# The sample tokens' mLSTM recurrence moved from a phase of its own into the head loop of the mLSTM phase, with y passed to the output projection through DRAM

## The reference, cut to what matters

```python
# prompt: 16 chunks of 64 tokens in the reference, state starts at zero
# sample: one chunk of 4 tokens for each of 8 sequences, state comes in as state_C, state_n, state_m
num = w_inter[..., None] * einsum('bhvk,bhjk->bhjv', c, qc) + einsum('bhjs,bhsv->bhjv', a, vc)
den = w_inter * einsum('bhk,bhjk->bhj', n, qc) + sum(a, axis=-1)
h = num / maximum(abs(den), exp(-mj))[..., None]
c_new = decay[..., None, None] * c + einsum('bhs,bhsv,bhsk->bhvk', wg, vc, kc)
n_new = decay[..., None] * n + einsum('bhs,bhsk->bhk', wg, kc)
# then, in the layer:
hc = head_rmsnorm(sigmoid(o) * h, hnorm)
x + (hc * silu(z)) @ w_out_a
```

## Time and profile before

| what | value |
|---|---|
| median of 3 runs | 1976.89 us (1974.68 to 1979.36) |
| the profiled execution | 1973.47 us, of which its span is 1971.8 us |
| TensorE busy over the span | 1775.7 us (90%) |
| VectorE / ScalarE / GpSimd busy | 1069.3 (54%) / 761.8 (39%) / 458.5 us (23%) |
| the head loop of the mLSTM phase | about 39 to 684 us |
| the sample phase | about 684 to 801 us |
| output projection, then the rest | 801 us to the end |

### The profile page before, as it was taken

How to read it: one execution, slowest core, us unless ns; L and a number is a source line. 1 busy time by engine, 2 the same in 40 slices (tenths; PEclk the granted TensorE clock), 3 DMA queues, 4 the chain that set the end, 5 groups by cost and what they waited for, 6 DMA issues and landing times. The chain is left out here.

```text
span 1971.8 us, 37984 instructions
## 1 busy us (share of the span) xinstructions
PE 1775.7 (90%) x12147; PEld 1584.6 (80%) x12147; DVE 1069.3 (54%) x2885; ACT 761.8 (39%) x2040; POOL 458.5 (23%) x863
## 2 busy tenths in 40 slices
PE   4899999999999768797999999999999688888698
PEld 4789999999899756576998999999999666666385
DVE  4653443543543444425666666666665466767543
ACT  5333333333333212313335344344353356666511
POOL 1121221221212212012324334244242100101101
PEclk8899999999999966798999999999999798989799
DMA  5203213213121033612111211211200267676532
GB/s 156 68 3 67 38 30 68 36 32 68 7 61 15 4 90 95 206 43 92 34 35 43 55 34 32 66 34 32 65 13 11 95 234 265 237 273 232 159 127 87
DMA packets 146957, 164.83 MB, mean 84 GB/s; under 512 B 12730, under 2 KB 118042, under 8 KB 146898
## 3 DMA queue, kind: packets, MB, share of 16 engines
q1 hardware_dynamic: 142594, 159.85, 27.0%
q0 software_dynamic: 1184, 4.23, 0.8%
q10 hardware_dynamic: 3120, 0.01, 0.1%
HBM read 138.69 MB, written 25.37 MB: 83 GB/s over the span
## 5 line engine op out<-in xcount | busy, mean ns | idle before, releaser
L820 PE MATMUL PS<-WH,XH 128*128 128x384 f32 (+3 forms) x1152 | 370.0, 321 | 0.0
L820 PE MATMUL PS<-WL,XH 128*128 128x384 f32 (+3 forms) x1152 | 357.3, 310 | 0.0
L820 PE MATMUL PS<-WH,XL 128*128 128x384 f32 (+3 forms) x1152 | 357.3, 310 | 0.0
L820 PEld LDWEIGHTS PS<-WH,XH 128*128 128x128 f32 (+1 forms) x1152 | 208.8, 181 | 4.5
L820 PEld LDWEIGHTS PS<-WL,XH 128*128 128x128 f32 (+1 forms) x1152 | 208.8, 181 | 4.1
L820 PEld LDWEIGHTS PS<-WH,XL 128*128 128x128 f32 (+1 forms) x1152 | 208.2, 181 | 4.6
L1890 PE MATMUL PD<-WH,XH 128*128 128x256 f32 (+1 forms) x576 | 169.9, 295 | 2.9 <-PEq L142 2.9
L1890 PE MATMUL PS<-WH,XH 128*128 128x256 f32 (+1 forms) x576 | 168.3, 292 | 0.2 <-ACT WORK L1625 0.2
L1890 PE MATMUL PD<-WL,XH 128*128 128x256 f32 (+1 forms) x576 | 164.2, 285 | 0.0
L1890 PE MATMUL PD<-WH,XL 128*128 128x256 f32 (+1 forms) x576 | 163.7, 284 | 0.0
L1890 PE MATMUL PS<-WL,XH 128*128 128x256 f32 (+1 forms) x576 | 162.3, 282 | 0.0
(11 more groups left out here) (361 smaller groups left out, 4152.7 us busy)
## 6 DMA issues: line engine op xcount, KB each, us to landing
RAW<-in_cache_k SPq DMA_DIRECT2D x64, 512.0 KB, 4.6
WORK<-in_cache_v SPq DMA_DIRECT2D x64, 512.0 KB, 4.5
RAW<-in_w_in_a SPq DMA_DIRECT2D x40, 512.0 KB, 6.2
RAW<-in_w_in_b SPq DMA_DIRECT2D x16, 512.0 KB, 6.3
RAW<-in_w_kv SPq DMA_DIRECT2D x16, 512.0 KB, 5.3
out<-RAW SPq DMA_DIRECT2D x12, 512.0 KB, 3.8
out<-WORK SPq DMA_DIRECT2D x12, 512.0 KB, 3.2
WORK<-in_x_prompt SPq DMA_DIRECT2D x8, 512.0 KB, 4.4
```

The lines of the kernel that those rows point to most:

```text
L820: last = nc.tensor.matmul(bank[0:rows, 0:n], x[:, k, tt], reg(w)[:, k, :], start=(i == 0), stop=(i == 3 * KT - 1))
```

## The change

`mlstm_sample_phase` is gone. Its work for head h is cut into pieces that each engine runs inside sweep1 of head h + 1, at fixed blocks t; head 7, which has no next head, runs its pieces one after the other behind the loop (`last_head`). `SS` stays in SBUF and is no longer stored. The states are loaded to `CI` and updated in place, so the next load waits for the store. Since the space of `YT` now holds the sample buffers, each head's y is collected in `YS` (1056 columns), stored to DRAM by GpSimd (`s_store`, `d_yA`), and read back by `out_phase` along with the weights. SP's loop is peeled for head 0. In the diff, pieces that only copy or scale small tiles (`s_gates`, `s_inter`, `s_square`, `s_queries`, `s_divide`, `s_gate`) are left out; they hold the instructions of the old phase with other buffers.

```diff
+                        if first:
+                            sp.wait_ge(g_col, 1)
+                            sp.dma_start(GS[0:TS, :, :], d_G[:, SEQ:TOK].partition_broadcast(TS)).then_inc(b_k, 16)
+                            sp.dma_start(HNS, hnorm_a[0, :].partition_broadcast(P)).then_inc(b_k, 16)
+                        else:
+                            sp.wait_ge(b_st, 16 * h)
+                        sp.dma_start(CI, state_C[0, :, bass.ds(h, 1), :, :].rearrange("b a v k -> v (b a) k")).then_inc(b_c, 16)
                         if not last:
                             sp.wait_ge(lo1, KT * (h + 1))
                             load1(h + 1)
-                        sp.wait_ge(ss, h + 1)
-                        sp.dma_start(d_smA[:, :, bass.ds(h * P, P)], SS[0:TS, :, :]).then_inc(a_sst, 16)
...
+                            if before is not None:
+                                if t == 0:
+                                    tail(before)
+                                    s_gates(before)
+                                if t == 2:
+                                    s_state(before)
+                                if t == 6:
+                                    s_inter(before)
+                                if t == 7:
+                                    s_square(before)
...
+                    def s_state(h):
+                        act.wait_ge(b_qt, h + 1)
+                        act.activation(QT2, BK[4][:, 0:2 * TS].rearrange("p (a t) -> p a t", a=2), ACT.Copy)\
+                           .then_inc(b_qe, 1)
+                        act.wait_ge(b_ctp, h + 1)
+                        act.activation(CT[:, 0:4, 0:P], BK[5].rearrange("p (b v) -> p b v", b=4), ACT.Copy)
+                        act.activation(CT[:, 4:8, 0:P], BK[7].rearrange("p (b v) -> p b v", b=4), ACT.Copy).then_inc(b_cte, 1)
...
+                            if t == 3:
+                                s_gate(before)
+                        s_root(before)
...
+                    def s_root(h):
+                        pool.wait_ge(b_sq, h + 1)
+                        apart(pool)
+                        slinks.link(g.tensor_scalar(svar[0:TS, :], sss[0:TS, :], 4.0 / P, 16 * EPS, ALU.mult, ALU.add))
+                        g.tensor_tensor(srs[0:TS, :], svar[0:TS, :], neg_half[0:TS, :], ALU.pow).then_inc(b_rr, 1)
+                        pool.wait_ge(b_cn, h + 1)
+                        pool.dma_start(c_s[0, :, bass.ds(h, 1), :, :].rearrange("b a v k -> v (b a) k"), CI).then_inc(b_st, 16)
+                    def s_store(h):
+                        pool.wait_ge(b_yte, h + 1)
+                        pool.dma_start(d_yA[bass.ds(h, 1), :, :].rearrange("a p t -> (a p) t"), YS).then_inc(a_yst, 16)
+                    def last_head(h):
+                        s_gate(h)
+                        s_root(h)
+                        s_store(h)
+                        pool.wait_ge(b_nev, 1)
+                        pool.dma_start(n_s[0, :, :, :].rearrange("b h k -> (b h) k"), nN[0:DB * H, :]).then_inc(b_nst, 16)
+                        pool.wait_ge(b_st, 16 * H)
+                        pool.wait_ge(a_yst, 16 * H)
+                        pool.wait_ge(b_nst, 16)
+                    def sweep2(h, last, first=False):
+                        if not first:
+                            s_store(h - 1)
...
-                        v.tensor_copy(YT[:, bass.ds(h, 1), c * P:(c + 1) * P].rearrange("p a c -> p (a c)"),
-                                      BK[2 + c % 2][:, 0:P]).then_inc(tr_free[c % 2], 1)
+                        v.tensor_copy(YS[:, c * P:(c + 1) * P], BK[2 + c % 2][:, 0:P]).then_inc(tr_free[c % 2], 1)
...
+                    def s_weight(h):
+                        hh = bass.ds(h, 1)
...
+                        v.tensor_tensor(VW[0:TS, :, :],
+                                        SS[0:TS, 2, :].unsqueeze(1).to_broadcast([TS, DB, P]),
+                                        WG[0:TS, :].unsqueeze(2).to_broadcast([TS, DB, P]), ALU.mult).then_inc(b_vw, 1)
...
+                    def s_update(h):
+                        hh = bass.ds(h, 1)
+                        dve.wait_ge(b_ex, h + 1)
+                        dve.wait_ge(b_s, h + 1)
...
+                        v.tensor_tensor(nO[:, :, hh].rearrange("p b a -> p (b a)"), nM, BK[4][:, 64:64 + DB], ALU.add)
+                        v.scalar_tensor_tensor(sAT[0:TS, :], BK[4][0:TS, 0:TS], K_SCALE, sEX[0:TS, :],
+                                               ALU.mult, ALU.mult).then_inc(b_at, 1)
+                        dve.wait_ge(b_upd, h + 1)
+                        for s in range(DB):
+                            bank = BK[5] if s < 4 else BK[7]
+                            last_one = v.scalar_tensor_tensor(CI[:, s, :], CI[:, s, :],
+                                                              DEC[:, bass.ds(h * 2 * NT + NT + s, 1)],
+                                                              bank.rearrange("p (b k) -> p b k", b=4)[:, s % 4, :],
+                                                              ALU.mult, ALU.add)
+                        last_one.then_inc(b_cn, 1)
...
+                    def s_output(h):
+                        dve.wait_ge(b_rr, h + 1)
+                        dve.wait_ge(b_gz, h + 1)
+                        v.scalar_tensor_tensor(sY[0:TS, :], sU[0:TS, :], srs[0:TS, :], sGZ[0:TS, :],
+                                               ALU.mult, ALU.mult).then_inc(b_y, 1)
+                    def s_transposed(h):
+                        dve.wait_ge(b_yt, h + 1)
+                        v.tensor_copy(YS[:, SEQ:TOK], BK[4][:, 2 * P:2 * P + TS]).then_inc(b_yte, 1)
...
+                            if before is not None:
+                                if t == 0:
+                                    s_weight(before)
+                                if t == 2:
+                                    s_queries(before)
+                                if t == 4:
+                                    s_update(before)
+                                if t == 6:
+                                    s_divide(before)
+                                if t == 8:
+                                    s_output(before)
+                                    s_transposed(before)
...
+                                if t == 2:
+                                    dve.wait_ge(a_yst, 16 * h)
...
+                    def s_turn(h):
+                        pe.wait_ge(ss, h + 1)
+                        pe.wait_ge(cev, h + 1)
...
+                        for j in range(2):
+                            last = nc.tensor.transpose(BK[4][:, j * TS:(j + 1) * TS], SS[0:TS, j, :], ident[0:TS, 0:TS])
+                        last.then_inc(b_qt, 1)
+                        pe.wait_ge(b_c, 16 * (h + 1))
+                        for s in range(DB):
+                            bank = BK[5] if s < 4 else BK[7]
+                            last = nc.tensor.transpose(bank.rearrange("p (b v) -> p b v", b=4)[:, s % 4, :], CI[:, s, :], ident)
+                        last.then_inc(b_ctp, 1)
+                    def s_scores(h):
+                        pe.wait_ge(b_qe, h + 1)
+                        pe.wait_ge(b_wg, h + 1)
+                        nc.tensor.matmul(BK[4][0:TS, 0:TS], QT2[:, 1, :], QT2[:, 0, :], start=True, stop=True)
+                        nc.tensor.matmul(BK[4][:, 64:64 + DB], SS[0:TS, 1, :], WG[0:TS, :], start=True, stop=True)\
+                          .then_inc(b_s, 1)
+                        pe.wait_ge(b_vw, h + 1)
+                        pe.wait_ge(b_cte, h + 1)
+                        for s in range(DB):
+                            bank = BK[5] if s < 4 else BK[7]
+                            last = nc.tensor.matmul(bank.rearrange("p (b k) -> p b k", b=4)[:, s % 4, :], VW[0:TS, s, :],
+                                                    SS[0:TS, 1, :], start=True, stop=True)
+                        last.then_inc(b_upd, 1)
+                    def s_cell(h):
+                        pe.wait_ge(b_ini, 2)
+                        pe.wait_ge(b_at, h + 1)
+                        apart(pe)
+                        nc.tensor.matmul(BK[4][0:TS, 0:P + 1], sAT[0:TS, :], sVA[0:TS, 0:P + 1], start=True, stop=True)
+                        pe.wait_ge(b_qz, h + 1)
+                        for s in range(DB):
+                            last = nc.tensor.matmul(BK[6][0:TS, 0:P + 1], QZ[:, s * TS:(s + 1) * TS], CT[:, s, 0:P + 1],
+                                                    start=(s == 0), stop=(s == DB - 1))
+                        last.then_inc(b_cell, 1)
+                    def s_out(h):
+                        pe.wait_ge(b_y, h + 1)
+                        apart(pe)
+                        nc.tensor.transpose(BK[4][:, 2 * P:2 * P + TS], sY[0:TS, :], ident[0:TS, 0:TS]).then_inc(b_yt, 1)
...
-                            if t == 0 and before is not None:
-                                tail(before)
+                            if before is not None:
```

(20 more changed lines are left out.)

394 lines of the change are left out of this document (146 added, 248 removed).

## The result

The changed kernel takes 1944.79 us (median of 4 runs, 1941.53 to 1946.04), the kernel before 1975.79 in the same runs: ratio 0.9838, 95% interval 0.9819 to 0.9857, faster by 31.0 us. The ratios are taken over all runs of a set, so they differ a little from the quotients of the medians. The forecast was 1938, with 1924 to 1958 around it. Profiled execution: 1973.47 us before, 1944.36 after; span 1971.8 before, 1942.4 after.

The account below looks back on a forecast made before the run. TensorE was taken to bound the loops, and a 118 us chain of waits at half clock to lie between. 53.6 + 0.4 - 95.0 + 4.0 = -37.0 us gave 1939.9; forecast 1938, range 1924 to 1958.

Parts of the forecast that it names:

- The loop's price: Head loop: the sample's pieces and the wait at the turn cost 7.65 us per head, 53.6 for seven.
- The stretch of 118 us: Head loop's end to output projection's first load: falls from 118.0 to 23.0 us, head 7 alone remaining; -95.0.
- Loop, instructions: Sweep 1: 49 added TensorE instructions cost 6.0 us per head, bounded between 5.4 and 6.7.
- Loop, the turn: Sweep 1 to sweep 2: TensorE waits for y's chain through VectorE, 1.65 us per head, not under 1.2.
- the next product 0.05 later: At the turn: sweep 2's first product follows the end of VectorE's copy of y by 0.05 us.
- Cost at nothing: In the loop: VectorE, ScalarE and GpSimd work, stores and their waits stay hidden beside TensorE; no added time.
- The projection's start: Output projection: first product about 8.5 us after the first load instead of 4.44, y coming by DMA; +4.0.
- my row: DMA of y: a 512 KB store in the earlier profile lands 4.8 us after its issue.
- Rival A: Turns: idle TensorE drops to half clock, 1.7 to 3.4 us more each, 1950 to 1962 us; chance 0.14.
- Rivals B and C: Loop: y hand-over slips a block, 1983 us, 0.07; or more waits, in sweep or projection loads, near 1958, 0.06.

Follow-up runs that it names:

- r_before: The kernel before the change, run again unaltered: 1976.93 us.
- r_after: The changed kernel, run again unaltered: 1945.88 us.
- e3: Changed kernel with the eight state transposes of each head done twice: 1948.65 us, one run.
- e2: Changed kernel with y's transpose into another bank and TensorE waiting for VectorE's copy only ahead of the first cell: 1944.74 us.
- e10: As e2, but TensorE's seven heads of the loop written out without a loop: 1938.12 us, one run.
- e5: Changed kernel with eight more VectorE operations per head, into a free tile ahead of the state update: 1943.13 us, one run.
- e8: Changed kernel with each head's y stored twice, to two DRAM tensors, VectorE waiting for both: 1943.30 us, one run.
- e1: Changed kernel with the transpose of the sample's y and its copy moved behind the first projection of sweep 2: 1928.24 us.
- e6: Changed kernel with the last head's y kept in place and projected first, its state and n stored earlier: 1934.44 us.
- e4: Changed kernel with four more round trips between TensorE and VectorE at each turn: 1967.89 us, one run.
- e9: Changed kernel with y's transpose behind sweep 1's last projection, a late wait for its copy, and e6's end of the loop: 1923.55 us.

## Why the prediction was right, and where it was off

**Direction, mechanism and range were right.** The loop's price, the gain and the late start of the projection came where they were forecast; to the first output product the sum was -37.0 and -33.67 was measured. On the medians 31 to 32 us are left of 37. The median came out 7 to 8 us above the forecast 1938, of which 1.9 were given away by setting the forecast below the prediction's own 1939.9.

**The stretch of 118 us: right, and to the hundredth by luck.** -95.0 forecast, -95.01 measured. Of the parts of head 7 alone, what stands ahead of the outer products took 0.4 us more than forecast, outer and y products 7.8 us as one row (745.77 to 753.61, forecast 7.9), from there to the copied y 4.2 (forecast 4.8), from the copied y to the first load 6.7 (forecast 6.5): misses that cancel. Between r_before (116.96) and r_after (23.20) the same term is -93.76.

**Loop, instructions: 6.0 forecast, 6.19 measured.** The transpose of y stands in the turn, so the other 48 cost 0.129 each; e3 shows the pure pitch of transposes, 0.110. I put the difference, 0.9 us per head, down to the beginnings and ends of the pieces, for which I had taken 0.6; no run isolates it, and the outer products' own pitch is nearer 0.12 in the trace, so that it may be less.

**Loop, the turn: 1.65 forecast, 1.94 measured.** Of the change's own costs this is the most mis-sized term, 2.0 us over seven heads. The step that failed is "the next product 0.05 later": the copy ends at 605.76, the product starts at 606.25, 0.49 later; y, transpose and copy came 0.14 sooner than forecast and hid a part of that. I had priced what the engines hand to each other and not the loop's return, since the earlier trace rows show none; e2 and e10 showed that it is 0.6 us and open when TensorE has waited at that place. The Trainium skill, "Advanced Engine Details and Errata", section on control flow timing, gives an unconditional branch some 51 ns and a compare with a branch some 108; as an estimate of a return that would be 0.16 us. The runs show 0.6 for the return as a whole and 0.22 for the compare and branch that goes back, so here the measurement decides.

**Cost at nothing: right.** Period unchanged with more VectorE work (e5) and with twice the stores (e8), and no piece waits inside a sweep.

**The projection's start: +4.0 forecast, +3.34 measured**, as the first y was in use after 4.3 us and not 4.8. In the other profiles with this start it is +2.9 (e3) to +4.1 (e1), so the difference is within the scatter. By the rule of the Trainium skill that the prediction weighed ("DMA: Bandwidth & Descriptors", anatomy of one DMA, a fit for copies that GpSimd issues, so for the store and not for SP's load) 3.2 us were estimated for such a copy; in the loop a store of y takes 3.7 to 3.8 us from issue to landing, between the rule and my row.

**Rival A, the clock: not met in the changed kernel's profile, but nearer than its chance said.** In that profile the clock is 1.00 from 91 to 740 us. In r_after, e2, e5 and e6, with the same turn of about 2.2 us, it fell once, each time at the first turn, and the sweep 2 behind it took 53.9 instead of 52.4 us: 1.5 to 1.6 us. In e3 and e8 it didn't. Here is r_after's first turn and what follows:

```profile
176.30:178.60 2.30, 0.60 (x5) 0.31 (x4) 1.10 (x5) 0.37 (x1) 0.43 (x1) 1.00 0.56 167
178.60:183.50 4.90, 4.90 (x20) 4.90 (x21) 0.91 (x3) 0.80 (x2) 0.57 (x1) 0.65 0.86 245
```

At a turn of 4.64 us it fell seven times of seven (e4); at 1.49 and less never (e10, e9, e1). The Trainium skill, "TensorE: Matmul & The Clock Gate", section on psum-queue depth-cycling, tells of short idles between groups of products that make the clock swing. e4 agrees with it, seven turns of seven; the changed kernel's own turn agrees at most once in a profile. Why only the first turn is hit at 2.2 us stays open.

**Rivals B and C: refuted.** No hand-over slipped by a block, and the projection's loads were hidden: its first 192 products took 46.43 us from first to last start, 46.00 before.

**The rest of the miss.** From -37.0 to the -33.67 of the first output product: the loop 2.9, the last head's sweep 2 0.66, the start 0.48, the projection 0.66 the other way. The last head's sweep 2 takes 49.5 and 49.6 us in the two profiles before and 49.7 to 50.2 in those after that have the turn of 2.2 us, so a part of its 0.66 is real; I had put it at nothing, and its cause stays open. From -33.67 to the medians' -31.0 and -31.7 lie, as far as the profiles tell, the fall of the clock at the first turn, which r_after had and the first profile hadn't (1.6), and the removed stretch itself, 116.96 us in r_before and not 118.23; the rest is within the scatter of the later stages.

## What to carry to other kernels

Work moved beside a full engine cost that engine's time by the instruction and little else here, since what it needs is made a block ahead; the only wait that was left was the one at the loop's boundary, and it cost a quarter of the price. Don't let a bounding engine's last wait stand right ahead of a loop's return: put the dependent instruction behind queued work, as e1 and e9 did. And where a tile is stored and read back, look whether its last part already lies where the reader wants it.

## What the runs showed of the hardware that I had not expected

A loop's return costs TensorE 0.6 us when it has just waited and nothing is queued (0.85 to 0.25 us from the transpose to the next product, e2 to e10), 0.22 us of it the branch itself. It costs nothing that can be seen when work is queued ahead of it (0.21, e1): in the kernel before, the register instruction behind the branch ran more than 1.6 us ahead of the product that follows it. The label of an idle ("<-DVE") can name a releaser that had been done for half a microsecond: taking that releaser away changed 0.72 to 0.64. And a turn of 2.2 us, with two idles, lowered the clock at no more than one turn of a profile, while one of 4.6 us, with six idles of 0.9 us and less, lowered it at all seven.
